# Turning expert rows and results on VectorE in 32x32 blocks instead of on TensorE, in a routed mixture-of-experts layer

## The reference

```python
hf = h.reshape(n_tok, d)                       # 1024 x 1024
top_val, top_idx = lax.top_k(hf @ w_r + b_r, 4)  # 4 of 32 experts for each token
gates = softmax(top_val)
...
def expert_block(args):                        # for each expert, its tokens' rows xb
    u = xb @ w_in[e] + b_in[e]                 # 1024 -> 2048
    return _clamped_swiglu(u) @ w_out[e] + b_out[e]   # 1024 -> 1024
...
out[token] += ys * gate                        # summed over a token's 4 experts
```

## Time and profile before

| | |
|---|---|
| time, median of 3 runs | 1977.61 us (1976.02 to 1979.94) |
| span of the profiled execution | 1959.1 us; its own device time is not listed, the median lies 18.5 us above the span |
| mean granted TensorE clock | 0.997 |
| PE busy | 1923.4 us, 98% |
| DVE, ACT, POOL busy | 33%, 24%, 11% |
| DMA | 523.95 MB, 267 GB/s over the span |

### The profile page before, as it was taken

How to read it: one execution, slowest core, us unless ns; L and a number is a source line. 1 busy time by engine, 2 the same in 40 slices (tenths; PEclk the granted TensorE clock), 3 DMA queues, 4 the chain that set the end, 5 groups by cost and what they waited for, 6 DMA issues and landing times.

```text
span 1959.1 us, 50916 instructions
## 1 busy us (share of the span) xinstructions
PE 1923.4 (98%) x22971; PEld 1732.3 (88%) x22971; DVE 655.1 (33%) x1890; ACT 467.9 (24%) x1382; POOL 217.5 (11%) x250
## 2 busy tenths in 40 slices
PE   7999999999999999999999999999999999999997
PEld 4756765566999999999999999999999999999997
DVE  2655766665331212121222222222222222222224
ACT  3104544441121111111111112121211111122213
POOL 2003000001010101020201011101011110110002
PEclk9999999999999999999999999999999999999999
DMA  9880121116988888887969796969697988999986
GB/s 360 307 181 20 44 76 54 44 54 207 363 316 295 292 323 311 298 309 278 333 255 354 263 355 252 371 245 369 245 380 253 370 319 327 340 330 337 323 320 223
DMA packets 150208, 523.95 MB, mean 267 GB/s; under 512 B 10027, under 2 KB 15811, under 8 KB 149987
## 3 DMA queue, kind: packets, MB, share of 16 engines
q1 hardware_dynamic: 131186, 467.68, 65.7%
q0 software_dynamic: 17200, 52.59, 7.9%
q10 hardware_dynamic: 1600, 0.36, 0.1%
HBM read 485.34 MB, written 34.21 MB: 265 GB/s over the span
## 4 chain that ended last, share of the span: by engine, by line
PE 94%; DVE 2%; SPq 1%; DMA 1%; issue 1%; ACT 0%; POOL 0%; ACTq 0%; DVEq 0%; POOLq 0%
PE ps L1683 47%; PE ps L1721 24%; PE ps L1518 5%; PE ps L1466 4%; PE ps L1526 3%; PE ps L1671 2%; PE ps L1644 2%; PE ps L1444 2%; PE ps L1498 1%; PE ps L1462 1%; DMA ring<-in_w_qkv 1%; PE ps L1487 1%; SPq L416 0%; SPq L428 0%; PE ps L1415 0%
## 5 line engine op out<-in xcount | busy, mean ns | idle before, releaser
L1683 PE MATMUL ps<-U,ring 128*64 128x120 f32 (+11 forms) x13312 | 935.5, 270 | 1.7 <-issue 1.7
L1683 PEld LDWEIGHTS ps<-U,ring 128*64 128x64 f32 (+1 forms) x13312 | 923.1, 149 | 9.5 <-issue 7.9
L1721 PE MATMUL ps<-U,ring 128*64 128x120 f32 (+11 forms) x6656 | 468.4, 270 | 0.1
L1721 PEld LDWEIGHTS ps<-U,ring 128*64 128x64 f32 (+1 forms) x6656 | 461.4, 149 | 4.1 <-issue 3.4
L1253 DVE TENSOR_SCALAR U<-ps,U 128x120 f32<-128x120 f32 (+11 forms) x256 | 90.7, 354 | 1089.6 <-PE ps L1683 1089.6
L829 ACT ACTIVATE U<-U 128x120 f32<-128x120 f32 (+11 forms) x256 | 80.2, 313 | 889.7 <-DVE U L1253 889.7
L840 ACT ACTIVATE U<-ps,U,modT 128x120 f32<-128x120 f32 (+11 forms) x256 | 119.0, 465 | 286.8 <-PE ps L1721 286.7
L593 POOL DMA_INDIRECT acc_d<-U x43 | 43.2, 1005 | 849.5 <-DVE U L1245 845.8
L1518 PE MATMUL ps<-ring 128*128 128x512 f32 (+1 forms) x288 | 114.9, 552 | 0.0
L1518 PEld LDWEIGHTS ps<-ring 128*128 128x128 f32 x288 | 53.4, 190 | 54.4 <-issue 52.9
L815 ACT ACTIVATE U<-ps,modT,Af 128x120 f32<-128x120 f32 (+11 forms) x252 | 91.9, 469 | 9.2 <-PE ps L1656 9.2
(11 more groups left out here) (231 smaller groups left out, 1100.3 us busy)
## 6 DMA issues: line engine op xcount, KB each, us to landing
ring<-in_moe_w SPq DMA_DIRECT2D x191, 2048.0 KB, 11.1
U<-in_w_mod SPq DMA_DIRECT2D x8, 2048.0 KB, 12.2
ring<-in_w_mod SPq DMA_DIRECT2D x3, 2048.0 KB, 19.4
ring<-in_w_qkv SPq DMA_DIRECT2D x3, 2048.0 KB, 18.5
acc_d<-xr SPq DMA_DIRECT2D x10, 512.0 KB, 3.4
xr<-in_x SPq DMA_DIRECT2D x8, 512.0 KB, 9.5
ring<-in_w_o SPq DMA_DIRECT2D x2, 2048.0 KB, 8.6
xn_d<-U SPq DMA_DIRECT2D x8, 512.0 KB, 2.6
```

The source lines that it names most:

```text
L1683: last = pe.matmul(bank(j % 4)[lo:hi, s * 256:s * 256 + n], w[:, k, s, (j % 2) * P + lo:(j % 2) * P + hi], xT[:, k, 0:n], start=(k == 0), ...
L1721: last = pe.matmul(bank(m % 4)[lo:hi, 0:n], w[:, k, (m % 4) * P + lo:(m % 4) * P + hi], actT[:, k, 0:n], start=(k == 0), stop=(k == KT - 1))
```

## The change

- **Rows in.** `rows_transpose` is gone but for slot 0. VectorE turns 32x32 blocks: `turn_x` is one `dve.transpose` for each pair of partition quarters (from quarter a of `xg` to quarter q of `turned_x`), with all 8 feature tiles in it, 256 elements a partition, or 512 where a wide slot's second block also reaches quarter a. That is 16 a slot, 12 in slots 88 wide. `turned_x` has two buffers in `xr`, which is idle in this stage. ScalarE's `rows_scale` scales from there into `xT`.
- **Results back.** `rows_back` is gone but for slot 31 (`last_rows_back`). `turn_y` turns `yT` into `turned_y`, also in `xr`, and `rows_out` adds 1024 elements at once.
- **Where they stand.** On VectorE two y turns follow `activate(j - 1)` in each up step (four in the last slot), in even slots two turns of the next slot's rows besides, and at the end of an even slot all turns of the slot after next. `rows_out(r - 1)` moves from up step 1 (or 5) to the end of the loop, and to j = 4 in slot 31. POOL's gathers of rows move with them: an even slot gathers r + 2 and r + 3.
- **Banks and order of the down products.** Down products use banks 4 to 7 and no longer share with the up products. The first four banks get K steps 0 to 5, one bank after another, and then K steps 6 and 7 each; the other four as before.
- Some semaphores of the router stage are merged, with the same waits.

```diff
+def turns(r):
+
+    return [(a, 2 if P + 32 * a < WIDTHS[r] else 1, q) for a in range(P // 32) if 32 * a < WIDTHS[r] for q in range(P // 32)]
 
...
+        free_x = xr.rearrange("p t n -> p (t n)")
+        turned_y = free_x[:, 0:2048].rearrange("p (b m q d) -> p b m q d", b=2, m=KT, q=P // 32)
+        turned_x = free_x[:, 2048:6144].rearrange("p (v k b t) -> p v b k t", v=2, k=KT, b=2)
+        xg_blocks = xg.rearrange("p b (k q d) -> p b k q d", k=KT, q=P // 32)
+        yT_blocks = yT.rearrange("p m (b t) -> p b m t", b=2)
...
             gather_rows(0)
+            pool.wait_ge(s_xtp, FIRST_ROUNDS)
+            gather_rows(1)
             for r in range(E):
-                pool.wait_ge(s_xtp, x_done[r + 1])
-                if r + 1 < E:
-                    gather_rows(r + 1)
+                if r % 2 == 0 and r + 2 < E:
+                    pool.wait_ge(s_xv, r + 1)
+                    gather_rows(r + 2)
                 if r == 0:
                     pool.wait_ge(s_x1d, (TT + 2) * 16)
...
-                    pool.wait_ge(s_ye, y_done[r])
+                    pool.wait_ge(s_ye, gathers[r])
                     scatter_sums(r - 1)
                     gather_gates(r)
                     pool.wait_ge(s_sout, gathers[r] * 16)
                     gather_sums(r)
+                if r % 2 == 0 and r + 3 < E:
+                    pool.wait_ge(s_xv, r + 2)
+                    gather_rows(r + 3)
             for t in range(0, TT, 2):
...
+            def rows_scale(r):
+
+                act.wait_ge(s_xv, r)
+                for k in range(KT):
+                    if wide(r):
+                        both = turned_x[:, r % 2, :, k, :].rearrange("p b t -> p (b t)")
+                        rows = both[:, 0:WIDTHS[r]]
+                    else:
+                        rows = turned_x[:, r % 2, 0, k, 0:WIDTHS[r]]
+                    last = act.activation(xT[:, k, 0:WIDTHS[r]], rows, ACT.Identity, scale=Af[:, k:k + 1], bias=modT[:, 24 + k:25 + k])
                 last.then_inc(s_xT, 1)
...
-                    for q in range(x_rounds(r + 1)):
-                        rows_evacuate(r + 1, q)
+                    rows_scale(r + 1)
+                if r:
+                    act.wait_ge(s_yt, r)
                 for m in range(8):
                     if r == E - 1 and m < TT - 3:
                         final_squares(m + 3)
                     act.wait_ge(s_mm, r * 16 + 8 + m + 1)
-                    act.activation(yT[:, m, 0:n], bank(m % 4)[:, 0:n], ACT.Identity, scale=modT[:, 40 + m:41 + m],
+                    act.activation(yT[:, m, 0:n], bank(4 + m % 4)[:, 0:n], ACT.Identity, scale=modT[:, 40 + m:41 + m],
...
+            def turn_x(r, first, end):
+
+                dve.wait_ge(s_g, gathers[r + 1] * 16 - 16)
+                if r == 1 and first == 0:
+                    dve.wait_ge(s_x1d, (TT + 2) * 16)
+                if r > 2 and first == 0:
+                    dve.wait_ge(s_xT, x_ready(r - 2))
+                some = turns(r)[first:end]
+                for a, n, q in some:
+                    to, at = slice(32 * q, 32 * q + 32), slice(32 * a, 32 * a + 32)
+                    last = dve.transpose(turned_x[to, r % 2, 0:n, :, at], xg_blocks[at, 0:n, :, q, :])
+                if first + len(some) == len(turns(r)):
+                    last.then_inc(s_xv, 1)
+
+            def turn_y(r, first, end):
+
+                dve.wait_ge(s_me, r * 8 + 8)
+                if r and first == 0:
+                    dve.wait_ge(s_ye, gathers[r])
+                some = turns(r)[first:end]
+                for a, n, q in some:
+                    at, to = slice(32 * q, 32 * q + 32), slice(32 * a, 32 * a + 32)
+                    last = dve.transpose(turned_y[to, 0:n, :, q, :], yT_blocks[at, 0:n, :, to])
+                if first + len(some) == len(turns(r)):
+                    last.then_inc(s_yt, 1)
+
+            def rows_out(r):
+                dve.wait_ge(s_yt, r + 1)
+                for b, rows in blocks(r):
+                    dve.scalar_tensor_tensor(out=ysb[0:rows, b, :], in0=turned_y[0:rows, b].rearrange("p m q d -> p (m q d)"),
+                                             scalar=gate[0:rows, b:b + 1], in1=ysb[0:rows, b, :], op0=ALU.mult, op1=ALU.add)\
+                        .then_inc(s_ye, 1)
+
...
+                y_step = 4 if r == LAST_SLOT else 2
+                out_at = 4 if r == LAST_SLOT else 8
+                for j in range(9):
+                    if j < 8:
+                        up(j)
+                    if j >= 1:
+                        activate(j - 1)
+                    if r and y_step * j < len(turns(r - 1)):
+                        turn_y(r - 1, y_step * j, y_step * j + y_step)
+                    if r % 2 == 0 and 2 * j < len(turns(r + 1)):
+                        turn_x(r + 1, 2 * j, 2 * j + 2)
+                    if r and j == out_at:
+                        rows_gate(r - 1)
+                        rows_out(r - 1)
+                if r == 0:
+                    output_places()
+                if r % 2 == 0 and r + 2 < E:
+                    turn_x(r + 2, 0, len(turns(r + 2)))
...
-                pe.wait_ge(s_xT, x_done[r + 1])
+                pe.wait_ge(s_xT, x_ready(r))
...
+                    if r or j >= 4:
                         pe.wait_ge(s_je, r * 8 + j - 3)
-                    elif r:
-                        pe.wait_ge(s_me, r * 8 + j - 3)
...
-                    if r and j == back_behind(r):
-                        rows_back(r - 1)
-
-                if r + 1 < E:
-                    for q in range(x_rounds(r + 1)):
-                        rows_transpose(r + 1, q)
-                for m in range(8):
-                    if m % 4 == 0:
-                        pe.wait_ge(s_wl[4 + m // 4], loads_of(r, 4 + m // 4))
-                    if m < 4:
-                        pe.wait_ge(s_je, r * 8 + m + 5)
-                    else:
+
+                def down_product(m, k):
+                    w = piece(4 + m // 4).rearrange("p (k n) -> p k n", k=KT)
+                    for lo, hi in parts:
+                        last = pe.matmul(bank(4 + m % 4)[lo:hi, 0:n], w[:, k, (m % 4) * P + lo:(m % 4) * P + hi], actT[:, k, 0:n],
+                                         start=(k == 0), stop=(k == KT - 1))
+                    return last
+
+                pe.wait_ge(s_wl[4], loads_of(r, 4))
+                for m in range(4):
+                    if r:
                         pe.wait_ge(s_me, r * 8 + m - 3)
-                    w = piece(4 + m // 4).rearrange("p (k n) -> p k n", k=KT)
-                    for k in range(KT):
+                    for k in range(KT - 2):
                         if m == 0:
                             pe.wait_ge(s_act, r * 8 + k + 1)
-                        for lo, hi in parts:
-                            last = pe.matmul(bank(m % 4)[lo:hi, 0:n], w[:, k, (m % 4) * P + lo:(m % 4) * P + hi], actT[:, k, 0:n],
-                                             start=(k == 0), stop=(k == KT - 1))
+                        down_product(m, k)
+                for m in range(4):
+                    for k in range(KT - 2, KT):
+                        if m == 0:
+                            pe.wait_ge(s_act, r * 8 + k + 1)
+                        last = down_product(m, k)
+                    last.then_inc(s_mm, 1)
+                pe.wait_ge(s_wl[5], loads_of(r, 5))
+                for m in range(4, 8):
+                    pe.wait_ge(s_me, r * 8 + m - 3)
+                    for k in range(KT):
+                        last = down_product(m, k)
                     last.then_inc(s_mm, 1)
                     if r == E - 1 and m == 5:
-                        rows_back(r, (0,))
+                        last_rows_back(0)
```

167 lines of the change are left out of this document (65 added, 102 removed).

## The result

The changed kernel takes 1912.3 us (median of 4 runs, 1911.14 to 1915.14), the kernel before 1976.86 beside it (4 runs, 1976.02 to 1979.94): a ratio of 0.9675 [0.9661, 0.9689]. That is 64.6 us faster where 78.7 were forecast, inside the range and 13.3 us above the predicted 1899.

A forecast was written before the change was run, and what follows sets the result against it. The prediction took TensorE's instruction stream, busy 98% of the span, as the bound. Terms of -84.7 and +6 gave -78.7 us, a span of 1880.4, plus 18.5 to the median: 1899 us, range 1891 to 1918.

The forecast's parts named there:

- TensorE's turns leave: Turns in and back, 86.0 us, come off TensorE's stream except slot 31's own, kept at 1.3 us: -84.7 us.
- As long as nothing new makes PE wait: Condition for the stage: whatever leaves TensorE's stream comes off the span unless PE gets new waits; those looked for priced 0.
- PE idle under 5 us before slot 31: Sign expected in the changed trace: PE idle for less than 5 us ahead of the last slot.
- The 18.5 us between span and median: Difference of the earlier kernel's median over its profiled span, added to the predicted span of 1880.4 to give 1899 us.
- VectorE's turns: 968 turns of 0.41 and 0.68 us duration add 365 us to VectorE, 738 us in the stage: not a bound.
- rivals 1 and 3: Turns far slower than any row: 1934 us, chance 6%; VectorE bounding every slot, slower than before: 2087 us, chance 3%.
- Start of the down products: K steps 0 to 5 of four banks cover the last activations: 0 us, bounds 0 and 0.5 us per 88-wide slot.
- Weights and gathers: Late slots ask for 349 GB/s, 98% of the full-share rate, with some 18 us of cover: 0 us.
- rival 2: DMA becomes the bound in late slots through slower weights or row gathers: +5 to +20 us, 1912 us, chance 8%.
- The last slot: Slot 31 and tail: later `rows_out(30)` delays scatter, loads and squares, so PE waits: +5.2 us net, bounds 0 and +10.

The follow-up runs named there:

- c_half_loads: The changed kernel with only the first half of every weight piece loaded from slot 1 on: 1881.28 us, 0.9585 of the kernel before.
- j_after_again: The changed kernel run once more, unaltered, on chip 0: 1913.1 us, 0.9659 of the kernel before.
- d_tail: The changed kernel with, in the last slot alone, eight result turns a step and `rows_out(30)` at up step 2 instead of 4: 1889.84 us, 0.963 of before.
- e_straight_k: The changed kernel without the 6+2 order, each of the first four down banks taking its eight K steps in a row: 1953.83 us, 0.9948 of before.
- after: The changed kernel itself, in its first trace, against the kernel before: 1912.3 us, ratio 0.9675.

## Why the prediction was right, and by how much it was off

*TensorE's turns leave: right.* On chip 9 the stage without any hold-up of instructions is 1347.1 us (`c_half_loads`). The kernel before has 1433.05 there, 2.4 us of it pauses in slots 3 and 5 (34.47 and 34.66 us, where slot 1, as wide, takes 33.37); 1430.6 - 1347.1 = 83.5 us. The term for the stage was 84.7 - 1.0 for slot 31 (with 0.1 us for its starts) = 83.6. The premise, that in this stage time is the length of TensorE's stream, held for the kernel before.

*"As long as nothing new makes PE wait" is the step that failed.* I looked for waits behind VectorE, weights and gathers and priced each at 0, which was right for each; none appears ahead of slot 31. The new wait was for instructions. On chip 9 the pauses are 1363.1 - 1347.1 = 16.0 us, against 2.4 before: 13.6 us of the gain not delivered. On chip 0 they are 1380.5 - 1347.1 = 33 us: some 13 in the main of this kind, 20 of the second, whose cause isn't known. The prediction had "PE idle under 5 us before slot 31". Shown for the first kind: it goes with half the weight traffic, it goes with half as many products, though the weights flow, it stands a page of instructions apart and ends 1.2 to 1.5 us after a page has landed, a page's packet begins some 2 us later where data fill the DMA engines, and a pause comes in slot 1 of the kernel before as well when its TensorE has less to do. Not shown is why the turns in and back protected the narrow slots before; they pass more time per instruction (130 ns a turn against 38.6 ns a product), which fits. In this stage before, PE's stream had 3.5 per cent more matmuls and took 5.1 per cent longer than the changed kernel's on the same chip. The rivals of this explanation, VectorE's turns as such, the time of the gathers and the row transfers, account for 4 to 6 us each at most.

The Trainium skill, page "Runtime: NRT & Kernel Launch", section "Instruction fetch mechanics", has each engine fetch its instructions in pages of 256 by a DMA queue of its own and says the cost is mostly hidden. This case's trace agrees with the page size (254 products and weight loads), and with the cost being hidden in the wide slots and, with half the weights, everywhere. In the narrow slots under full traffic it isn't hidden: 6.3 us for a page that 88-wide half products use up in 4.9.

*The 18.5 us between span and median were misread.* I took them for what lies around a span. Every later run has 1.5 us there. The first trace of before (1959.1 us) is like those of chip 9, where the kernel takes 1963 us; the timed runs shown beside it, 1977 us, are like those of chip 0, 1981. The changed kernel has a difference of the same size: its stage takes 1379.6 and 1380.5 us where the kernel before was timed at 1977 and 1981 us, and 1363.1 on chip 9. As both kernels pay it, the sum came out as if the 18.5 us were an overhead. That is luck. In the changed kernel the difference is the second kind of pause (17.0 and 20.1 us against 0.0). Where the kernel before spends them isn't known, for no trace of it was had there; nor is what differs between the chips. The comparison of the two first traces (1959.1 and 1911.4, 47.7 us) would have put a loss of 31 us on the change; measured within one chip it is 14.

*VectorE's turns.* Duration right (0.41 and 0.68 us forecast, 436 and 699 ns measured). But they follow each other 0.45 and 0.71 us apart, without the 0.08 us of overlap that other rows have the earlier trace rows, so the stage has 798 us of VectorE instead of 738. It made no difference to PE: rivals 1 and 3 are out. Of the page of the Trainium skill that I weighed ("VectorE: DVE Perf Modes"), the table in "The three transpose paths" has VectorE the quicker one for bf16, 311 ns against 390. Here, in float32, it is the other way: 0.13 us for 128x128 on TensorE against two instructions of 0.44 (32 partitions by 256 elements are half of it). The page's rule for authors, TensorE for a 128x128 turn, agrees with that, and it doesn't matter, since VectorE's time is free and TensorE's is not.

*Start of the down products: term 0 right, and only thanks to the 6+2 order,* which hides 45 us of waits and the falls of the clock behind them.

*Weights and gathers: term 0 right,* rival 2 out. The late slots moved 343 GB/s at a share of 0.96, as forecast (0.97), and no wait on `ring` came.

*The last slot: the number right, the end of the chain not.* Forecast +5.2 us net, measured 59.8 - 54.2 = 5.6 (and 58.3 - 54.8 = 3.5 between the later pair, on two chips). The chain began in the forecast order: `rows_out` at +18.0 in the slot (19.2), scatter +19.6 (20.0), loads +25.1 (24.7), first square +28.5 (28.4), PE waiting 3.8 us for ScalarE at a down bank. But the forecast had the squares and VectorE's multiplications end last, at 48.4. They ended at 47.2, and PE's last turn, forecast for 46.5, ended at 48.8 and set the end. A cost that the forecast hadn't at all is in it: the granted clock fell to its lower level at 1887.5 us, during PE's wait, for 6.8 us, and 64 products took 6.01 us where the next 64 took 3.50:

```profile
1895.70 3.50 PE L1746 MATMUL ps<-U,ring 128*64 128x120 f32 x64
```

That is 2.5 us (1.6 in `j_after_again`), so that the sum came out is luck in part. `d_tail` shows that all of it could be avoided.

**The sum again, on chip 9** (the changed kernel's time there is an estimate from `d_tail` and the two tails): -83.5 (turns) + 13.6 (pauses) + 3.5 to 5.6 (tail) = -64.3 to -66.4; the changed kernel there is 1889.8 + 4.5 to 6.0, so 1894.3 to 1895.8, against 1962.7: -66.9 to -68.4.

## What to carry to other kernels

When work is taken off a full TensorE, ask what the stream becomes: short products back to back need instructions faster, and where transfers of data filled the DMA engines a page of some 127 products and their loads came 6.3 us after the last, 50 ns a product, against an estimated 3.9 us where they didn't. It is no fixed limit, since weights come in bursts: on chip 9 slots with 48.1 ns a product had no pause, slots with 44.8 ns lost 0.4 to 1.5 us beside 34.4, slots with 38.1 ns 1.9 to 4.5 beside 29.3, but slots 25 and 28, with 51.3 and 54.6 ns, lost 0.9 and 1.4 as well. Compare traces only within one chip, and check that span and timed runs of a kernel belong together before their difference is called an overhead. A move to an idle engine is paid for by cover elsewhere: here the order of 24 products ahead of the first one that needs the last activation carried 59 of the 70 us gained in the stage.

## What the runs showed of the hardware

- Waits on `issue` at TensorE, with a DMA share of 0.91 over the stage (`d_tail`) and none at 0.56 (`c_half_loads`), a page of 254 instructions apart. The packet with the next page (16 KB, about 1.0 us) began 3.2 to 3.8 us after a page's first product with the DMA engines busy and 1.1 to 1.6 us after it with them nearly idle, and TensorE went on 1.2 to 1.5 us after it had landed.
- After a wait of 2.0 us or more TensorE's granted clock went to 0.50 for 3.4 us in seven slots of `e_straight_k`, and for 6.8 us in the last slot of `after`, where 64 products took 6.01 us instead of 3.50. Not every such wait did it: in slots 8, 26 and 30 of `e_straight_k` the clock stayed up.
- The same program takes longer on one chip than on another at the same granted clock (0.993 to 0.998): the kernel before 1980.6 against 1962.7 us, the changed kernel's stage 1380.5 against 1363.1, where one stretch of every narrow slot from 1 to 23 loses 1.0 to 2.3 us on the slower chip alone.
- A float32 product that fills 128 columns takes 112 ns for 88 as for 120 columns of data, while two half products take 76 at 88 (29.27 us for 384 pairs) and 103 at 120 (39.36 us).
- A turn on VectorE of 256 float32 elements on 32 partitions takes 436 ns, of 512 elements 699, and turns don't overlap each other.
